# Routing a mixture of experts from the raw residual: where the norm is applied, how the first pair's rows are picked, and where the block arithmetic stands

## The chip, the cores and the metric

One core of one Trainium2 chip runs the whole step in one launch. The time is device microseconds of one execution. TensorE (PE), VectorE (DVE), ScalarE (ACT), GpSimd (POOL) and SyncE (SP) have instruction streams of their own and meet only in semaphores; SP here issues the large loads. TensorE's clock has two levels, 2.4 GHz (the profile's granted clock 1.00) and 1.2 GHz (0.50).

## The reference, cut to what matters

The part that the change touches begins with the merge of the two attention branches and ends with the experts' first blocks:

```python
x = x + jnp.einsum('btd,de->bte', gate_nsa * y_nsa + gate_diff * y_diff, w_out)
h = rmsnorm(x, norm_ffn).reshape(b * t, D_MODEL)          # 320 rows (256 + 64) of 1024
...
logits = (h @ w_router + b_router).astype(jnp.float32)    # 32 experts
top_val, top_idx = lax.top_k(logits, TOP_K)               # 4 per row
gates = jax.nn.softmax(top_val, axis=-1)
...
gu = x_e @ w_gate_up[e] + b_gate_up[e]                    # 1024 -> 2048, f32
act = (up + 1.0) * gate * jax.nn.sigmoid(SWIGLU_ALPHA * gate)
return act @ w_down[e] + b_down[e]                        # 1024 -> 1024, f32
```

All is f32. An expert's weights are 8.39 MB (gate and up) and 4.19 MB (down), 32 experts are 403 MB.

## The kernel before, in words

The kernel is written engine by engine; each engine's order is that of its Python function, and nothing reorders it. The 320 rows stand in three tiles t = 0, 1, 2 of 128, 128 and 64 rows.

**Merge and projection.** `branch_products` gives six (tile, half) pieces v, DVE multiplies and adds each (`m_done`), TensorE transposes it (`tp`, 4 transposes), ACT takes the left half out of PSUM and DVE the right one, into `mT`. Then five output projections `out_proj(v)` of 8 f32 matmuls each (v = 4 holds both halves of the 64-row tile) end in `z_full`.

**Norm and router.** DVE adds each piece to the residual `x5` (`x2_done`), ACT squares and takes the root, DVE writes the normed rows `hn[t]`; TensorE transposes them, the gains `gffn` are multiplied in on the way out of PSUM (`hT6`), and 24 matmuls (`logits`) give the logits.

**Dispatch.** DVE finds the four experts of each row (`max`, `max_index`, the one-hot `oh`, the mask `msk16`). 12 small matmuls with triangles and ones give each row's rank within its expert (`rk`) and the experts' counts (`cc`). From these DVE works out `dest`, the slot of each (row, choice) in blocks of `BS` = 64 rows, with the arithmetic for experts that fill more than one block (`steps_over`, `nb`, `ovb`). A `pick` matrix of a pair of experts, rows by 128 slots, has a 1 where a row goes to a slot: `pick_rows` builds it from `dest` in 12 DVE instructions. `picked(p)` multiplies it with `hn` (pick is the stationary operand, 6 matmuls of 512 columns), ACT copies the result to `hg`, `rows_t` transposes it in 8 pieces, and `rows_out` multiplies by the gains into `hTm`, two halves of 64 slots, one for each expert of the pair.

**Experts.** For each pair of experts: `gate_up(i, u)` (32 matmuls, weights streamed as the moving operand, plus 4 for the biases), DVE and ACT apply the activation, `acts_t` transposes, `down(i, u)` (16 matmuls plus 2), and the results are added back to `x5` through a `spread` matrix. `slot_marks` gives the row numbers and gates of the slots. Both gate-and-up buffers of the pair are one buffer `gu_w` in four chunks of two k-steps: SP may load chunk c of the next expert when the matmuls that read it are done (`e_used`). SP's queue:

```python
sp.wait_ge(z_full, 5)
for h in range(2):
    down_weights(sp, 0, 0, h)
sp.wait_ge(bias_ready, 1)
for h in range(2):
    down_weights(sp, 1, 1, h)
for c in range(4):
    sp.wait_ge(e_used, c + 1)
    gate_up_weights(sp, 1, c)
...
for c in range(4):
    sp.wait_ge(e_used, 5 + c)
    gate_up_weights(sp, 2, c)
```

So expert 0's gate-and-up weights come right behind the branch products, the first four down pieces behind the last projection, expert 1's behind the k-steps of `gate_up(0, 0)`, and expert 2's behind those of `gate_up(0, 1)`; every later load is released in the same way.

## Time and profile before

| | us |
|---|---|
| median of 3 runs | 1601.38 (1599.15 to 1603.20) |
| the profiled execution, its own time | 1600.19 |
| its span in the trace | 1598.5 |
| TensorE matmul busy in it | 1453.9 (91%) |
| DVE, ACT, POOL busy | 483.1, 288.2, 101.9 |
| bytes moved | 507.55 MB, mean 318 GB/s |

The time of the profiled execution is 1.7 us above its span; both belong to the same run. Times in the rows are from the start of the span. An f32 matmul leaves two records in the trace (a transpose or a bf16 matmul leaves one), so counts there are twice those of the code. Busy time says little about limits here: what counts is which stream the last pieces of work wait for.

### The profile page before, as it was taken

The page shows a single profiled execution, that of the slowest core. Times are in us where ns is not written, and L with a number is a line of the kernel's source. Part 1 is how long each engine was busy: PE and PEld are TensorE (multiplying, and loading weights), DVE is VectorE, ACT ScalarE, POOL GpSimd, SP SyncE. Part 2 cuts the span into 40 slices and gives each one's busy share as a digit, 9 for nine tenths or more (in the row PEclk, how much of TensorE's full clock was granted, in tenths as well). Part 3 has the DMA queues.
Part 4 walks back from the last instruction along what each step waited for, and adds up shares of the span by engine and source line. Part 5 has one row for each costly group of instructions (what it writes and reads, how often), then busy time and mean ns, then how long its engine had stood idle before and what let it go on. Part 6 is the DMA issues. An engine that isn't in the chain of part 4 may idle for free.

```text
span 1598.5 us, 21368 instructions
## 1 busy us (share of the span) xinstructions
PE 1453.9 (91%) x7498; PEld 655.7 (41%) x7498; DVE 483.1 (30%) x1097; ACT 288.2 (18%) x613; POOL 101.9 (6%) x217
## 2 busy tenths in 40 slices
PE   5998988988878995899999999999999999999996
PEld 3446554765656443333333333333333333333332
DVE  1113463334343355323132132122222212313214
ACT  2003333333343211010110111110110110010102
POOL 1002002432410000000000000000000000000000
PEclk9997999989989996899999999999999999999998
DMA  7217735665766855589999999999999999999993
GB/s 245 105 53 202 263 93 183 207 204 158 240 179 196 251 220 210 210 361 430 427 428 430 428 427 431 428 427 430 428 427 430 428 427 430 429 427 428 430 426 123
DMA packets 97210, 507.55 MB, mean 318 GB/s; under 512 B 28898, under 2 KB 43714, under 8 KB 72034
## 3 DMA queue, kind: packets, MB, share of 16 engines
q1 hardware_dynamic: 89090, 483.28, 75.7%
q0 software_dynamic: 8064, 23.60, 4.6%
q8 instruction: 25, 0.41, 0.1%
q14 instruction: 31, 0.25, 0.0%
HBM read 500.35 MB, written 10.62 MB: 320 GB/s over the span
## 4 chain that ended last, share of the span: by engine, by line
PE 64%; DMA 18%; DVE 5%; SPq 5%; issue 5%; ACT 2%; DVEq 0%; ACTq 0%
PE PS L1269 20%; DMA arena<-in_w_gate_up 18%; PE PS L1296 9%; PE PS L1243 6%; PE PS L343 5%; PE PS L1870 3%; PE PS L1235 2%; PE PS L1190 2%; PE PS L529 2%; PE PS L1049 2%; SPq L410 2%; PE PS L599 2%; SPq L415 1%; PE PS L352 1%; PE PS L1814 1%
## 5 line engine op out<-in xcount | busy, mean ns | idle before, releaser
L1269 PE MATMUL PS<-arena 128*64 128x512 f32 x2048 | 459.1, 597 | 25.7 <-DMA arena<-in_w_gate_up 23.4
L1269 PEld LDWEIGHTS PS<-arena 128*64 128x64 f32 x2048 | 142.3, 137 | 311.7 <-issue 262.5
L1296 PE MATMUL PS<-arena 128*64 128x512 f32 x1024 | 227.4, 597 | 3.2 <-DVE arena L1689 2.3
L1648 DVE TENSOR_SCALAR arena<-PS 128x512 f32<-128x512 f32 x32 | 22.1, 691 | 501.4 <-PE PS L1278 485.7
L1296 PEld LDWEIGHTS PS<-arena 128*64 128x64 f32 x1024 | 72.4, 138 | 151.3 <-issue 148.6
L529 PE MATMUL PS<-arena 128*128 128x128 f32 (+1 forms) x624 | 98.8, 300 | 37.5 <-ACT arena L762 13.7
L1243 PE MATMUL PS<-arena 128*128 128x512 f32 (+1 forms) x192 | 94.4, 635 | 9.4 <-DVE arena L1596 8.1
L529 PEld LDWEIGHTS PS<-arena 128*128 128x128 f32 (+1 forms) x624 | 72.8, 150 | 61.3 <-ACT arena L762 19.7
L1235 PE MATMUL PS<-arena 128*128 128x512 f32 (+1 forms) x192 | 79.4, 618 | 6.0 <-ACT arena L1438 6.0
L343 PE MATMUL PS<-arena 128*128 128x512 f32 (+1 forms) x192 | 79.6, 576 | 0.6 <-ACT arena L2055 0.6
L1153 POOL COPY arena<-arena 96x64 bf16 (+1 forms) x34 | 7.9, 234 | 1042.0 <-PE PS L1301 954.8
L1618 DVE TENSOR_TENSOR arena<-PS,arena 128x512 f32<-128x512 f32 x34 | 23.3, 687 | 165.1 <-PE PS L1251 160.1
L1423 ACT ACTIVATE arena<-arena 128x512 f32<-128x512 f32 x32 | 20.1, 630 | 273.0 <-DVE arena L1648 273.0
L762 ACT ACTIVATE arena<-PS 128x512 f32<-128x512 f32 (+2 forms) x96 | 51.1, 545 | 77.9 <-PE PS L529 77.5
L1430 ACT ACTIVATE arena<-PS 128x512 f32<-128x512 f32 x32 | 19.1, 597 | 248.0 <-PE PS L1286 248.0
L1437 ACT ACTIVATE arena<-PS 64x512 f32<-64x512 f32 x32 | 18.9, 590 | 230.8 <-PE PS L1301 229.2
L1243 PEld LDWEIGHTS PS<-arena 128*128 128x128 f32 (+1 forms) x192 | 35.4, 197 | 61.2 <-issue 52.9
L1870 PE MATMUL PS<-arena 128*128 128x512 f32 x128 | 59.9, 621 | 0.0
L599 PE MATMUL PS<-arena 128*128 128x252 f32 x256 | 55.1, 376 | 0.0
L343 PEld LDWEIGHTS PS<-arena 128*128 128x128 f32 x192 | 37.2, 195 | 42.4 <-issue 40.1
L2037 ACT ACTIVATE arena<-PS 128x512 f32<-128x512 f32 (+12 forms) x50 | 23.4, 489 | 153.0 <-PE PS L343 54.5
L599 PEld LDWEIGHTS PS<-arena 128*128 128x128 f32 x256 | 48.3, 190 | 5.6
(279 smaller groups left out, 1318.9 us busy)
## 6 DMA issues: line engine op xcount, KB each, us to landing
arena<-in_w_gate_up SPq DMA_DIRECT2D x128, 2048.0 KB, 22.2
arena<-in_w_down SPq DMA_DIRECT2D x64, 2048.0 KB, 21.8
arena<-in_w_in SPq DMA_DIRECT2D x9, 2048.0 KB, 11.7
arena<-in_cache_diff_k SPq DMA_DIRECT2D x64, 256.0 KB, 4.6
arena<-in_cache_diff_v POOLq DMA_DIRECT2D x64, 256.0 KB, 4.3
arena<-in_cache_sel_kv SPq DMA_DIRECT2D x64, 128.0 KB, 2.2
arena<-in_cache_cmp_kv POOLq DMA_DIRECT2D x64, 64.0 KB, 4.2
arena<-in_cache_cmp_kv SPq DMA_DIRECT2D x64, 64.0 KB, 2.8
```

What stands on the lines that cost most here:

```text
L343: last = nc.tensor.matmul(bank(proj_bank(q, 2 * s + t))[:, 0:w], xnT[:, k, 128 * t:128 * t + 128], chunk_at(j)[:, k, 0:w], start=(k == 0), ...
L410: return eng.value_load(ptab[0:1, bass.ds(i * (2 * NPAGE) + (b * NPAGE + pg), 1)], min_val=0, max_val=NPOOL - 1)
L529: last = nc.tensor.transpose(bank(n % 2)[0:c, col:col + r], src, order[0:r, 0:r])
L599: last = nc.tensor.matmul(bank(2)[:, 4 * NCC * c:4 * NCC * (c + 1)], w1[:, c, l, :], cmpT[:, 2 * c:2 * c + 2, :, l % (CS // 2), 2 * l // C ...
L762: copy = lambda d, s: nc.scalar.activation(d, s, ACT.Copy)
L1049: last = nc.tensor.matmul(bank(BRANCH_BANK[v] + half)[p:p + r], src[:, k, 128 * t:128 * t + r], w[:, k, 512 * nh:512 * nh + 512], start=(k ...
L1190: last = nc.tensor.matmul(bank(2 + v)[p:p + r], mT[:, k, 128 * t:128 * t + r], w_out[:, k, 512 * nh:512 * nh + 512], start=(k == 0), stop= ...
L1235: last = nc.tensor.matmul(out, spread[:, 128 * t:128 * t + ROWS[t]], ypair[:, 512 * h:512 * h + 512], start=True, stop=True)
L1243: last = nc.tensor.matmul(bank(h), pick[0:ROWS[t], t], hn[t][0:ROWS[t], 512 * h:512 * h + 512], start=(t == 0), stop=(t == 2))
L1269: last = nc.tensor.matmul(bank(2 + role + 2 * u)[64 * h:64 * h + 64], hTm[:, k, BS * u:BS * u + BS], gu_w[:, k, D * role + 512 * h:D * rol ...
L1296: last = nc.tensor.matmul(bank(6 + u)[64 * h:64 * h + 64], aT[u][:, c % 4, 64 * (c // 4):64 * (c // 4) + 64], down_w[u][c // 4][:, c % 4, ...
L1870: last = nc.tensor.matmul(bank(7), xnT[:, k, 128 * t:128 * t + 128], chunk_at(j)[:, k], start=(k == 0), stop=(k == KD - 1))
```

## The change

Six edits, all between the branch products and the second pair of experts:

1. **Router from raw rows.** TensorE transposes `x5` itself (`x2_t`), not the normed rows. The router weights are multiplied by the gains once (`wr` times `gffn_kp`, a second load of the norm's weights in another layout; `w_router` is loaded in that layout too, rows of 128 bytes in place of 1 KB). The factor 1/rms is applied to the logits in one DVE instruction, `scalar_tensor_tensor`. ACT writes `hn`, off that path.
2. **Order of the tiles.** Merge, transposes and projections are interleaved; the projections run in the order v = 0, 1, 4, 2, 3 (`Z_ORDER`) and the tiles in the order 0, 2, 1 (`T_ORDER`), so that tiles 0 and 2 are transposed, routed and ranked before the last projection ends.
3. **First pair from ranks.** `pick` of the first pair compares each row's rank in experts 0 and 1 with the slot number (`marked_ranks`, `first_rows`); neither `dest` nor the block arithmetic is needed.
4. **Rows stationary.** `first_pick` takes `hn` as the stationary operand and `pick` as the moving one, 8 matmuls of 128 columns for each tile, so the picked rows come out transposed, in banks 4 and 5 that two matmuls with zeros have opened; the ACT copy and the 8 transposes of the first pair are gone.
5. **Block arithmetic later.** `blocks_over`, `dest`, the pair marks and the block lists stand on DVE behind `rows_out` of the first pair; TensorE runs `blocks_over` between k-steps of `gate_up(0, 0)` and `slot_marks` behind `rows_t(1)`, and reads the number of extra pairs behind `down(0, 0)`.
6. **Small ones.** The bias splitting on DVE (`bias16`, `mid16`) is moved into the merge; two dummy activations load ACT's tables early; some buffers have other addresses.

```diff
             load(sp, "late", gffn, io["norm_ffn"].rearrange("a (p k) -> p (a k)", k=KD))
-            load(sp, "late", wr, io["w_router"][0].rearrange("(p k) e -> p k e", k=KD))
+            load(sp, "late", gffn_kp, io["norm_ffn"].rearrange("a (k p) -> p (a k)", p=128), allow_slow_non_contiguous=True)
+            load(sp, "late", wr, io["w_router"][0].rearrange("(k p) e -> p k e", p=128))
...
+            def first_pick(t, ks=range(KD)):
+
+                pe.wait_ge(hn_ready, T_ORDER.index(t) + 1)
+                pe.wait_ge(pick_ready, T_ORDER.index(t) + 1)
+                for k in ks:
+                    last = nc.tensor.matmul(bank(4 + k // 4)[:, 128 * (k % 4):128 * (k % 4) + 128], hn[t][0:ROWS[t], 128 * k:128 * k + 128], pick[0:ROWS[t], t],
+                                            start=False, stop=(t == 1 and k % 4 == 3))
                 return last
...
+            out_proj(2)
+            for half in range(2):
+                x2_t(2, half)
+            for half in range(2):
+                logits(0, half)
+            out_proj(3, range(3))
+            x2_t(1, 0)
+            for half in range(2):
+                logits(2, half)
+            out_proj(3, range(3, 7))
             pe.wait_ge(msk_ready, 1)
...
+            out_proj(3, range(7, KD))
+            logits(1, 0)
+            first_pick(0, range(4))
+            x2_t(1, 1)
+            first_pick(0, range(4, KD))
+            logits(1, 1)
+            first_pick(2)
+            pe.wait_ge(msk_ready, 2)
...
+            first_pick(1).then_inc(x_tp, 1)
...
-            picked(0)
-            rows_t(0)
             pe.wait_ge(bias_ready, 1)
             pe.wait_ge(x_out, 1)
-            gate_up(0, 0)
-            slot_marks()
-            m_out_done(pe, 12)
-            pe.wait_ge(blocks_ready, 1)
-            more = pe.value_load(novi[0:1, 0:1], min_val=0, max_val=NBLK_OVER // 2)
+            gate_up(0, 0, blocks_over, 1)
             pe.wait_ge(x_out, 2)
             picked(1)
             rows_t(1)
+            slot_marks()
             gate_up(0, 1, lambda: acts_t(0, 0))
             down(0, 0)
+            pe.wait_ge(blocks_ready, 1)
+            more = pe.value_load(novi[0:1, 0:1], min_val=0, max_val=NBLK_OVER // 2)
...
+            def marked_ranks(t):
+
+                st.own()
+                op(V.scalar_tensor_tensor, rank1[:, t], bank(3 if t % 2 else 2)[:, NE * t:NE * t + NE], 1.0, msk16[:, NE * t:NE * t + NE], ALU.add, ALU.mult)
+
+            def first_rows(t, p):
+
+                st(V.tensor_tensor(pick[:, t].rearrange("p (e s) -> p e s", e=2), slot1.unsqueeze(1).to_broadcast([128, 2, BS]),
+                                   rank1[:, t, 2 * p:2 * p + 2].unsqueeze(2).to_broadcast([128, 2, BS]), ALU.is_equal), pick_ready if p == 0 or t == 2 else None)
...
+            past(dve, x_tp, 1)
+            for u in range(2):
+                rows_out(st, u, 4)
```

How the instructions stand on TensorE before, from the projections to the block arithmetic's two products (L1190 is a projection, L1171 a transpose, L1201 a logit product, L1223 and L1225 ranks and counts, L1228 and L1229 the two products; the picked rows, six of 512 columns, and their eight transposes follow; the number behind x is how many such instructions follow each other):

```order
L1190 MATMUL PS<-arena 128x512 x32
L1171 MATMUL PS<-arena 128x128 x8
L1190 MATMUL PS<-arena 64x512 x16
L1171 MATMUL PS<-arena 128x128 x8
L1201 MATMUL PS<-arena 128x32 x8
L1171 MATMUL PS<-arena 128x64 x8
L1201 MATMUL PS<-arena 128x32 x8
L1201 MATMUL PS<-arena 64x32 x8
L1223 MATMUL PS<-arena 128x32 x9
L1225 MATMUL PS<-arena 32x1 x3
L1228 MATMUL PS<-arena 128x32
L1229 MATMUL PS<-arena 128x1
```

The same engine after the change, from k-steps 3 to 6 of the last projection to the last ranks; two small count products and the last eight `first_pick` follow (L1198 projection, L1177 transpose, L1213 logits, L1271 the zeros, L1222 ranks, L1237 `first_pick`):

```order
L1198 MATMUL PS<-arena 128x512 x4
L1271 MATMUL PS<-arena 128x512 x2
L1222 MATMUL PS<-arena 128x32 x3
L1198 MATMUL PS<-arena 128x512
L1213 MATMUL PS<-arena 128x32 x4
L1237 MATMUL PS<-arena 128x128 x4
L1177 MATMUL PS<-arena 128x128 x4
L1237 MATMUL PS<-arena 128x128 x4
L1213 MATMUL PS<-arena 128x32 x4
L1237 MATMUL PS<-arena 128x128 x8
L1222 MATMUL PS<-arena 128x32 x3
```

Only a third of the logits and of the picking stands behind the last projection product now, and no product of 512 columns.

DVE behind the rank matmuls before (L1558 takes the ranks out of PSUM; L1522 is the helper `op` of the block arithmetic, L1597 and L1596 are `pick_rows` of the first pair):

```order
L1558 COPY arena<-PS 128x128
L1522 COPY arena<-PS 32x1
L1522 TENSOR_SCALAR arena<-arena 32x1
L1522 SCALAR_TENSOR_TENSOR arena<-arena 32x1 x3
L1569 COPY arena<-arena 32x128
L1522 TENSOR_SCALAR arena<-arena 128x32
L1522 SCALAR_TENSOR_TENSOR arena<-arena 128x32 x3
L1522 TENSOR_SCALAR arena<-arena 128x96
```

And after, behind the last rank matmuls (L1567 is `op` now, L1654 `first_rows`, L1679 the gates' subtraction, L1699 `rows_out`):

```order
L1567 SCALAR_TENSOR_TENSOR arena<-PS,arena 128x32
L1654 TENSOR_TENSOR arena<-arena 128x128
L1679 TENSOR_TENSOR arena<-arena 128x12
L1683 COPY arena<-PS 128x2x32
L1567 COPY arena<-PS 32x1
L1567 TENSOR_SCALAR arena<-arena 32x1
L1567 SCALAR_TENSOR_TENSOR arena<-arena 32x1 x3
L1694 COPY arena<-arena 32x128
L1699 TENSOR_TENSOR arena<-PS,arena 128x8x64 x2
L1654 TENSOR_TENSOR arena<-arena 128x128 x3
```

Two instructions now stand between the last ranks and the last pick matrix, and the arithmetic on `dest` has gone behind the rows of the first pair.

## Rows read from the trace of the kernel before

**Rows 1.** The page: the span, and GB/s in its 40 equal slices.

```profile
span 1598.5 us, 21368 instructions
...
GB/s 245 105 53 202 263 93 183 207 204 158 240 179 196 251 220 210 210 361 430 427 428 430 428 427 431 428 427 430 428 427 430 428 427 430 429 427 428 430 426 123
```

**Rows 2.** Windows: stretch, busy by engine, then granted clock, DMA share, GB/s.

```profile
612.00:624.00 12.00, 10.88 (x61) 10.43 (x60) 3.75 (x17) 3.36 (x9) 0.41 (x2) 0.50 1.00 429
...
628.00:632.00 4.00, 1.01 (x4) 0.93 (x4) 3.46 (x18) 0.00 (x0) 0.00 (x0) 0.50 0.02 8
...
680.00:684.00 4.00, 4.00 (x22) 1.62 (x22) 0.69 (x1) 0.00 (x0) 0.00 (x0) 1.00 0.01 4
...
684.00:688.00 4.00, 4.00 (x21) 1.40 (x18) 0.00 (x0) 0.00 (x0) 0.00 (x0) 1.00 0.75 262
...
1100.00:1500.00 400.00, 383.96 (x1662) 133.35 (x1660) 94.60 (x197) 40.71 (x69) 3.28 (x14) 1.00 1.01 428
```

**Rows 3.** Timeline of SP's queue: start, duration, load.

```profile
606.91 2.04 SPq L1068 DMA_DIRECT2D arena<-in_w_down  x4
...
656.64 0.33 SPq L1065 DMA_DIRECT2D arena<-in_w_gate_up  x1
...
684.28 0.33 SPq L1065 DMA_DIRECT2D arena<-in_w_gate_up  x1
```

**Rows 4.** Timeline of TensorE from the projections to `gate_up(0, 1)`.

```profile
567.75 1.02 PE L1171 MATMUL PS<-arena 128*128 128x128 f32 x8 [3.03 <-DVE arena L1484]
...
599.78 7.09 PE L1190 MATMUL PS<-arena 128*64 128x512 f32 x32
...
617.41 5.47 PE L1201 MATMUL PS<-arena 128*128 128x32 f32 x32
...
626.91 0.76 PE L1223 MATMUL PS<-arena 128*128 128x32 bf16 x9 [4.04 <-DVE arena L1551]
...
638.55 8.55 PE L1243 MATMUL PS<-arena 128*128 128x512 f32 x12 [8.14 <-DVE arena L1596]
...
651.25 15.65 PE L1269 MATMUL PS<-arena 128*64 128x512 f32 x64 [2.32 <-issue]
...
667.27 3.01 PE L1259 MATMUL PS<-arena 128*128 128x52 f32 x24
...
671.54 7.28 PE L1243 MATMUL PS<-arena 128*128 128x512 f32 x12 [1.26 <-issue]
...
679.51 1.15 PE L1251 MATMUL PS<-arena 128*128 128x128 f32 x8 [0.69 <-ACT arena L1413]
...
680.59 7.09 PE L1269 MATMUL PS<-arena 128*64 128x512 f32 x32
```

**Rows 5.** Timeline of TensorE elsewhere: the same kinds of work at full clock.

```profile
207.37 1.16 PE L1902 MATMUL PS<-arena 128*128 128x128 f32 x8 [0.75 <-ACT arena L2037]
...
221.00 3.58 PE L1902 MATMUL PS<-arena 128*128 128x128 f32 x16 [2.60 <-ACT arena L2037]
...
717.82 5.61 PE L1243 MATMUL PS<-arena 128*128 128x512 f32 x12
...
731.95 1.98 PE L1235 MATMUL PS<-arena 128*128 128x512 f32 x4 [0.26 <-ACT arena L1438]
...
788.14 1.98 PE L1235 MATMUL PS<-arena 128*128 128x512 f32 x4 [0.26 <-ACT arena L1438]
```

**Rows 6.** Timeline of DVE: bias split, first of the choice, last of the marks, `rows_out`.

```profile
571.96 3.35 DVE L1491 TENSOR_TENSOR arena<-arena 96x3072 f32<-96x3072 f32 x1
...
623.01 0.23 DVE L1540 TENSOR_TENSOR arena<-PS,arena 128x64 f32<-128x64 f32 x1 [3.16 <-PE PS L1201]
...
642.21 0.64 DVE L1612 TENSOR_SCALAR arena<-arena 128x104 f32<-128x104 f32 x3
...
650.47 1.28 DVE L1618 TENSOR_TENSOR arena<-PS,arena 128x512 f32<-128x512 f32 x2
```

**Rows 7.** The last of three loads of `b_down`, issued at 539.0: time to landing.

```profile
DMA to landing us min/median/max: 13.9/13.9/13.9
```

More of the change, by code:

```diff
@@ new lines, in pe_merge @@
+            out_proj(2)
[5 more added lines that the diff above has]
+            x2_t(1, 0)
+            for half in range(2):
+                logits(2, half)
+            out_proj(3, range(3, 7))
+            pe.wait_ge(msk_ready, 1)
+            for h in range(2):
+                nc.tensor.matmul(bank(4 + h), ones16[0:32], zero16, start=True, stop=False)
+            ranks(0, 0)
@@ new lines, in pe_merge @@
+            ranks(2, 0)
+            ranks(2, 2).then_inc(rk_full, 1)
+            out_proj(3, range(7, KD))
[6 more added lines that the diff above has]
+            pe.wait_ge(msk_ready, 2)
+            for s in T_ORDER:
+                ranks(1, s)
+            for s in T_ORDER:
+                total(s)
+            for s in T_ORDER:
+                last = count(s)
```

348 lines of the change are left out of this document (200 added, 148 removed).

## Prediction

> **What bounds the kernel now.** I read the page first, then the windows from 600 us on, then the timelines of SP, TensorE and DVE over that stretch. The page's GB/s row has two parts: uneven until slice 18, then 426 to 431 in every slice but the last [rows 1]. The window from 1100 to 1500 says why: the DMA share is 1.01 at 428 GB/s while TensorE is busy 383.96 of 400 us [rows 2]. The experts' weights are the bound there. A pair of experts moves 25.17 MB, at 428 GB/s 58.8 us; TensorE needs 56.2 us for a pair, from the combine at 731.95 to the one at 788.14 [rows 5]. TensorE has 2.6 us a pair to spare and follows the loads.
>
> So the end is set by when the stream of weights becomes unbroken, plus the bytes still to come. SP's timeline and the 4 us windows give that moment. The first four down pieces are issued at 606.91 and are in by 628, where the queue falls to 8 GB/s; expert 1's first chunk waits for `gate_up(0, 0)` and is issued at 656.64; from 680 to 684 the engines move 4 GB/s, because expert 2's first chunk waits for the second k-step of `gate_up(0, 1)`, and is issued at 684.28 [rows 2, 3]. From there on nothing breaks. Behind that chunk stand 30 experts' weights, 377.5 MB, which the change leaves alone. What it is worth is therefore how much earlier than 684.28 the second k-step of `gate_up(0, 1)` ends, as long as the loads in front of it are done.
>
> TensorE's timeline from 607 shows what stands before it: logits at 617.41, ranks at 626.91 after 4.04 us of waiting, the first pair's rows at 638.55 after 8.14 us of waiting for DVE's `pick_rows`, the gate products at 651.25, marks at 667.27, `gate_up(0, 1)` at 680.59 [rows 4]. From 612 to 624 the granted clock is 0.50, the 1.2 GHz level, after the wait that followed the last projection [rows 2].
>
> **The change, part by part.** Three stretches, each against the trace.
>
> *A, to the last projection product.* Before, TensorE ran dry at 564.72 (567.75 less the wait of 3.03) with the branch products and three of six transposes done [rows 4]; the projections ended at 606.9. Now it has work throughout. Left at 564.7 are three transposes of four pieces (8 take 1.02 to 1.15, so 0.55 each: 1.7), five projections at 7.05 (7.09 for the one at full clock: 35.2), five transposes of `x5` (2.8), the logits of tiles 0 and 2 (32 records; 24 like them take 3.01 in `slot_marks`, so 0.125 each: 4.0), and the zeros and three ranks (an estimate of 0.8 from nine such in 0.76 at the low clock) [rows 4]. Sum 44.5, end 609.2, 2.3 us later than before. What lies beside it: the bias split on DVE, two instructions of 3.35 and three shorter, now stands between the merges. DVE waits for the bias loads there, and `merge(3)` to `merge(5)` are queued behind. The last landed at 539.0 + 13.9 = 552.9 [rows 7]; the split's first half (1.75 + 3.35 [rows 6]) ends about 558, the last merge about 572, when TensorE wants it. The new `gffn_kp` load and the cut-up `w_router` stand ahead of the bias in the queue. If they cost up to 4 us, TensorE waits 1 to 2 us; below, nothing.
>
> The Trainium skill, "DMA: Bandwidth & Descriptors", Specifications, puts line rate at 512 bytes a piece or more, and both new loads are below it (4 and 128 bytes). That speaks against the layout; the price by this trace stays inside the 4 us above, and no row here shows the page's threshold.
>
> *B, from there to the first gate product.* Before: 606.9 to 651.25, 44.3 us. Now TensorE's list is half the logits of tile 1 (1.0), half of `first_pick(0)` (8 records of 128 columns: 1.16 [rows 5]), a transpose (0.55), the other half (1.16), the logits' other half (1.0), `first_pick(2)` (2.3): 7.2, to 616.4. DVE's choice for tile 1 runs under `first_pick(2)`: for three tiles it took 3.9 (623.01 to the ranks' start at 626.91), for one I take 1.7, as its compare and reduce shrink with the tiles [rows 4, 6]; it may cost the full 3.9, then TensorE waits 1.6 (it ends at 614.1 + 3.9 in place of 616.4). Ranks, totals and counts: 1.0. DVE marks and compares: two instructions near 0.23 and 0.3, with issue 0.6. `first_pick(1)` 2.3. `rows_out` of the first half 0.64, with issue 0.75 [rows 6]. Start at 616.4 + 1.0 + 0.6 + 2.3 + 0.8 = 621.1. B is 11.9 us where it was 44.3. Gone from the path are the block arithmetic and `pick_rows` (627.67 to 638.55, 10.9 us), six products of 512 columns (8.55), a copy and eight transposes (from 647.1, 4.15 with DVE's rows), and most of the logits and transposes (611 to 623).
>
> *C, from the first gate product to the second k-step of `gate_up(0, 1)`.* Before 651.25 to 684.28, 33.0 us. Now 14.1 (twice 7.09) for the gate products, 0.6 for the two products of the block arithmetic, 0.4 biases, 5.6 for `picked(1)` at full clock [rows 5], 0.7 until ACT's copy, 1.15 transposes, 3.0 marks, 3.5 for two k-steps: 29.0. The first gate products took 15.65, 1.55 over twice 7.09, as the clock was partly low [rows 4]; I keep half, 0.8. End of C: 621.1 + 29.8 = 650.9. The register read ahead of `picked(1)`, a wait of 1.26 [rows 4], goes behind `down(0, 0)`, where TensorE is ahead of the loads and it costs nothing.
>
> The arithmetic moved behind `rows_out` is hidden if the marks are ready before `slot_marks`. Before, DVE took from the ranks' end at 627.67 to 642.85 for all of it, `pick_rows` too: 15.2 us [rows 4, 6]. Begun behind the second `rows_out` (621.8) and 1.4 us of `first_rows` and gates, it is ready by 638.4; TensorE comes to `slot_marks` at 621.1 + 22.6 = 643.7. The cover is 5 us at least, and more by the `pick_rows` that are gone; without it each late microsecond would be one on the path.
>
> *The loads.* Four down pieces from 609.2 take 8.39 MB / 428 GB/s = 19.6, to about 629; expert 1's chunks follow without a break, their matmuls being done from 625 on, to about 649. Expert 2's first chunk is issued at 650.9: a gap of 2 us is left of one of 28 and one of 8.
>
> *The sum.* 684.3 - 650.9 = 33.4 us. The profiled execution took 1600.19 (span 1598.5), so 1566.8; the median of the runs shown, 1601.38, is 1.2 above it, so 1568.0.
>
> **The rivals.** *Low clock through B.* The granted clock was 0.50 from 612 to 624 although TensorE was busy 10.88 of 12 us with logits and transposes [rows 2]: such work did not raise it. If it also lets it fall, `first_pick` costs 3.58 for 16 records in place of 2.3 [rows 5]: 2.6 for two of them, 0.5 for the rest, 0.8 more in the first gate products, 1.7 in `picked(1)`. Gain 27.8, time 1573.6. Against it: B begins at full clock and its waits are 0.6 to 0.8 us, where the low stretch before began behind the wait that followed the projections' end at 606.87 [rows 4]. The Trainium skill, "TensorE: Matmul & The Clock Gate", PE-mode transpose, says a transpose doesn't count as busy for the clock; that would favour this rival, and the row from 612 to 624 agrees. Chance 0.2.
>
> *A longer chain.* B is 30 hand-overs. Half a dozen of them 0.5 late, DVE's choice at its upper bound (1.5), the bias late (1.5): 6 us, 1574. Chance 0.12.
>
> *The loads cap it.* If TensorE is quicker than I sum, expert 2 can't be loaded before 649, or 647 if the projections end at 607 as before. Gain at most 37, time 1564.4. That is the near edge of my own case.
>
> *The wait only moves.* If the marks came 15 us later than summed (a DVE wait on `ov_full` or the exponential's table load in the wrong place), `slot_marks` would hold `gate_up(0, 1)`; a late mark of 10 to 15 beyond the cover leaves a gain of 18 to 23, 1578 to 1583. The order speaks against it: `blocks_over` stands at the second k-step, 4 us in. Chance 0.05.
>
> *Slower.* The loop's buffers (`hTm`, `g1` to `av`, `aT`, `ypair`) have other addresses. If that slowed TensorE or the landing weights so that a pair took over 58.8 + 33.4/15 = 61.0 us, the gain would be spent; TensorE's 56.2 would have to grow by 4.8. At 62 us a pair the time is 1568 + 15 × 3.2 = 1616. The loop's instructions are the same, so 0.03. That the order does not free the path at all (1600) gets 0.02.
>
> **The numbers.** My own case, 1564 to 1571, has 0.58. The range 1562 to 1578 reaches from the cap with 2 us of scatter (the runs shown differ by 4) over the cold clock and the longer chain, and leaves out under 0.2. A change under 0.3%, 4.8 us, can't be told from none here. Faster 0.95, same 0.02, slower 0.03.
>
> **What would show it.** Right: the first gate product (L1336) near 621, `gate_up(0, 1)` near 647, the load of expert 2's first chunk near 651 and no window under 400 GB/s behind it; the granted clock 1.00 to about 615; the last projection product near 609; DVE's marks ready before 640. Wrong: a window with 0.50 between 605 and 625 (low clock); TensorE waiting more than 1 us on DVE behind the ranks (long chain); pairs longer than 58.8 us in the loop (slower); a gap in the loads behind 651.

## The result, and the profile after

The changed kernel took 1558.53 us (median of 4 runs, 1556.62 to 1561.83), the kernel before 1600.27 (4 runs, 1596.43 to 1603.20): ratio 0.9743, 95% interval 0.9714 to 0.9772, 41.7 us less. Forecast were 1568.0 us and a range of 1562 to 1578. The sign was right, the time lies 3.5 us below the range. The profiled execution took 1560.01 us, its span 1558.0, 40.5 less than the span of before. Of all executions in this document one stands far off, 5113.32 us of six for the kernel with the load early alone; the time given for it is the median of the other five.

The page after, the span and GB/s in 40 slices (as [rows 1]) and the costliest group, the gate products, with its idle time at the end:

```profile
span 1558.0 us, 21396 instructions
...
GB/s 252 108 54 191 266 98 156 199 238 170 222 160 233 244 281 192 414 429 427 429 429 427 429 429 427 429 429 427 429 429 427 429 429 427 429 429 427 428 429 128
...
L1336 PE MATMUL PS<-arena 128*64 128x512 f32 x2048 | 457.7, 596 | 24.3 <-DMA arena<-in_w_gate_up 23.5
```

Counted from 0, the full rate begins in slice 17, with 414 GB/s already in slice 16; before it began in slice 18, with 361 in slice 17. Of TensorE's 24.3 us of idle time ahead of gate products 23.5 are put down to the weights (23.4 of 25.7 before): they still bound the loop. The windows, with the columns of [rows 2]:

```profile
612.00:616.00 4.00, 3.31 (x16) 3.12 (x15) 1.35 (x7) 1.43 (x2) 0.00 (x0) 0.63 1.02 438
616.00:620.00 4.00, 3.86 (x19) 1.55 (x19) 3.42 (x16) 0.00 (x0) 0.00 (x0) 1.00 0.97 418
...
644.00:648.00 4.00, 4.00 (x22) 1.18 (x18) 0.00 (x0) 0.00 (x0) 0.00 (x0) 1.00 0.82 299
...
1100.00:1500.00 400.00, 384.10 (x1674) 132.99 (x1672) 98.02 (x202) 40.03 (x68) 3.02 (x13) 1.00 1.01 428
```

The two holes in the stream, from 628 and from 680 before, have become one short one: 299 GB/s from 644 to 648. From 1100 to 1500 the rate is the same, 428 GB/s. The granted clock is 0.63 on average from 612 to 616, just ahead of the first gate product, and 1.00 from 616. SP's timeline (as [rows 3]): down pieces, expert 1's first chunk, expert 2's first chunk.

```profile
604.06 1.94 SPq L1073 DMA_DIRECT2D arena<-in_w_down  x4
...
619.82 0.33 SPq L1070 DMA_DIRECT2D arena<-in_w_gate_up  x1
...
644.95 0.33 SPq L1070 DMA_DIRECT2D arena<-in_w_gate_up  x1
```

Expert 2's first chunk is issued at 644.95 in place of 684.28, 39.3 us earlier; the gain of the span is 40.5. TensorE's timeline (as [rows 4]; L1198 projection, L1177 transpose, L1213 logits, L1237 `first_pick`, L1336 gate product, L1326 `slot_marks`):

```profile
561.72 0.66 PE L1177 MATMUL PS<-arena 128*128 128x128 f32 x4
562.21 7.03 PE L1198 MATMUL PS<-arena 128*128 128x512 f32 x16
569.18 0.71 PE L1177 MATMUL PS<-arena 64*128 64x64 f32 x8
569.82 14.15 PE L1198 MATMUL PS<-arena 128*128 128x512 f32 x48
583.90 1.09 PE L1177 MATMUL PS<-arena 128*128 128x128 f32 x8
584.83 7.03 PE L1198 MATMUL PS<-arena 128*128 128x512 f32 x16
591.79 0.71 PE L1177 MATMUL PS<-arena 64*128 64x64 f32 x8
592.43 1.97 PE L1213 MATMUL PS<-arena 128*128 128x32 f32 x16
594.24 2.82 PE L1198 MATMUL PS<-arena 128*128 128x512 f32 x6
596.89 0.60 PE L1177 MATMUL PS<-arena 128*128 128x128 f32 x4
597.42 1.12 PE L1213 MATMUL PS<-arena 128*64 128x32 f32 x16
598.47 3.70 PE L1198 MATMUL PS<-arena 128*128 128x512 f32 x8
...
602.90 1.13 PE L1198 MATMUL PS<-arena 128*128 128x512 f32 x2
603.87 0.97 PE L1213 MATMUL PS<-arena 128*128 128x32 f32 x8
...
611.74 3.57 PE L1237 MATMUL PS<-arena 128*128 128x128 f32 x16 [0.70 <-DVE arena L1654]
616.14 3.65 PE L1336 MATMUL PS<-arena 128*64 128x512 f32 x16 [0.83 <-issue]
...
620.25 10.52 PE L1336 MATMUL PS<-arena 128*64 128x512 f32 x48
...
638.42 2.91 PE L1326 MATMUL PS<-arena 128*128 128x52 f32 x24
641.26 7.09 PE L1336 MATMUL PS<-arena 128*64 128x512 f32 x32
```

The waits of 4.04 and 8.14 us that stood ahead of ranks and picked rows in [rows 4] are gone, and so is a third one of before, ahead of the transposes of the normed rows (TensorE's timeline of before):

```profile
611.08 2.10 PE L1171 MATMUL PS<-arena 128*128 128x128 f32 x8 [4.21 <-ACT arena L1388]
```

Two of 0.70 and 0.83 are left. DVE's marks are ready at 628.7, 9.7 us ahead of `slot_marks` at 638.42, and DVE alone waited for the bias loads (DVE's timeline of after):

```profile
551.21 1.76 DVE L1567 CAST arena<-arena 96x3072 bf16<-96x3072 f32 x1 [2.50 <-DMA arena<-in_b_down]
...
628.11 0.64 DVE L1752 TENSOR_SCALAR arena<-arena 128x104 f32<-128x104 f32 x3
```

### The profile page after: what moved, and what is told of

It reads as the page before. It is cut to its first block, busy times and chain, and to the rows that moved or that the text cites. A ratio compares the mean times of both kernels' runs of the same rounds, so it can differ in the third digit from the quotient of the medians.

```text
span 1558.0 us, 21396 instructions
## 1 busy us (share of the span) xinstructions
PE 1437.8 (92%) x7528; PEld 650.1 (42%) x7528; DVE 475.2 (31%) x1084; ACT 292.1 (19%) x609; POOL 101.8 (7%) x217
## 4 chain that ended last, share of the span: by engine, by line
PE 69%; DMA 19%; DVE 5%; ACT 3%; issue 3%; SPq 1%; ACTq 0%; DVEq 0%
PE PS L1336 21%; DMA arena<-in_w_gate_up 18%; PE PS L1363 9%; PE PS L1310 5%; PE PS L343 5%; PE PS L599 3%; PE PS L529 3%; PE PS L2000 3%; PE PS L1302 3%; PE PS L1198 2%; PE PS L1054 2%; PE PS L352 1%; PE PS L572 1%; PE PS L1944 1%; ACT arena L762 1%
## 5 line engine op out<-in xcount | busy, mean ns | idle before, releaser
L1336 PE MATMUL PS<-arena 128*64 128x512 f32 x2048 | 457.7, 596 | 24.3 <-DMA arena<-in_w_gate_up 23.5
L1336 PEld LDWEIGHTS PS<-arena 128*64 128x64 f32 x2048 | 141.3, 137 | 308.9 <-issue 259.5
L529 PEld LDWEIGHTS PS<-arena 128*128 128x128 f32 (+1 forms) x624 | 73.5, 151 | 61.2 <-ACT arena L762 20.9
L1302 PE MATMUL PS<-arena 128*128 128x512 f32 (+1 forms) x192 | 79.4, 618 | 6.0 <-ACT arena L1506 6.0
L1310 PE MATMUL PS<-arena 128*128 128x512 f32 (+1 forms) x180 | 84.2, 609 | 0.0
L343 PE MATMUL PS<-arena 128*128 128x512 f32 (+1 forms) x192 | 78.6, 571 | 0.6 <-ACT arena L2185 0.6
L1699 DVE TENSOR_TENSOR arena<-PS,arena 128x512 f32<-128x512 f32 x34 | 23.3, 687 | 164.5 <-PE PS L1318 157.0
L2167 ACT ACTIVATE arena<-PS 128x512 f32<-128x512 f32 (+12 forms) x50 | 23.4, 488 | 151.2 <-PE PS L343 53.4
```

The source lines that it names most:

```text
L343: last = nc.tensor.matmul(bank(proj_bank(q, 2 * s + t))[:, 0:w], xnT[:, k, 128 * t:128 * t + 128], chunk_at(j)[:, k, 0:w], start=(k == 0), ...
L529: last = nc.tensor.transpose(bank(n % 2)[0:c, col:col + r], src, order[0:r, 0:r])
L1302: last = nc.tensor.matmul(out, spread[:, 128 * t:128 * t + ROWS[t]], ypair[:, 512 * h:512 * h + 512], start=True, stop=True)
L1310: last = nc.tensor.matmul(bank(h), pick[0:ROWS[t], t], hn[t][0:ROWS[t], 512 * h:512 * h + 512], start=(t == 0), stop=(t == 2))
L1336: last = nc.tensor.matmul(bank(2 + role + 2 * u)[64 * h:64 * h + 64], hTm[:, k, BS * u:BS * u + BS], gu_w[:, k, D * role + 512 * h:D * rol ...
L2167: copy = lambda d, s: nc.scalar.activation(d, s, ACT.Copy)
```

## How the span divides

Four points cut every trace into stretches that can be compared: the last DVE addition ahead of the merge (L942), the issue of the down pieces (the last projection product's end), the first gate product, the end of the span. The first of them, DVE's timeline, of before and then of the first, second and third run of the changed kernel:

```profile
532.05 0.43 DVE L942 TENSOR_TENSOR arena<-arena 128x256 f32<-128x256 f32 x1
```

```profile
529.82 0.43 DVE L942 TENSOR_TENSOR arena<-arena 128x256 f32<-128x256 f32 x1
```

```profile
534.64 0.43 DVE L942 TENSOR_TENSOR arena<-arena 128x256 f32<-128x256 f32 x1
```

```profile
531.88 0.43 DVE L942 TENSOR_TENSOR arena<-arena 128x256 f32<-128x256 f32 x1
```

The six edits of the change stand behind that point, and the changed kernel alone shows 4.8 us of scatter there. All kernels, in us. Time and ratio are from the timed runs, each ratio against the kernel before as it was timed beside it (1600.27 with the first run, 1598.96, 1599.70 and 1599.84 with the later ones); the stretches are from the one profiled run of each. A starts at the merge here.

| kernel | time | ratio, 95% | merge to down issue (A) | to first gate product (B) | from it to the end |
|---|---|---|---|---|---|
| before | 1600.27 | | 74.9 | 44.3 | 947.3 |
| changed | 1558.53 | 0.9743 [0.9714, 0.9772] | 74.2 | 12.1 | 941.9 |
| changed, second | 1562.82 | 0.9765 [0.9745, 0.9785] | 74.2 | 10.5 | 941.8 |
| changed, third | 1561.85 | 0.9763 [0.9749, 0.9776] | 74.2 | 10.5 | 942.2 |
| delay ahead of the gate product | 1569.01 | 0.9808 [0.979, 0.9826] | 74.2 | 17.6 | 941.9 |
| delay behind `down(0, 0)` | 1566.93 | 0.9801 [0.978, 0.9822] | 74.3 | 12.1 | 945.3 |
| arithmetic first | 1572.01 | 0.9825 [0.9806, 0.9845] | 74.2 | 20.9 | 943.1 |
| router from normed rows | 1566.78 | 0.9799 [0.9781, 0.9816] | 73.8 | 15.7 | 941.8 |
| projections first | 1570.30 | 0.9815 [0.9798, 0.9831] | 68.1 | 26.1 | 942.0 |
| rows moving | 1568.65 | 0.9807 [0.9791, 0.9824] | 73.6 | 18.1 | 941.8 |
| second half moved up, load early | 1560.98 | 0.9761 [0.9745, 0.9777] | 74.2 | 10.5 | 941.1 |
| three parts undone | 1583.01 | 0.9905 [0.9885, 0.9926] | 73.2 | 32.9 | 942.5 |
| `down(0, 0)` moved up, load early | 1560.62 | 0.9759 [0.9745, 0.9774] | 74.3 | 11.9 | 938.7 |
| load early alone | 1562.58 | 0.9766 [0.9751, 0.978] | 74.3 | 12.1 | 941.9 |

The 40.5 us of the two spans are 2.2 ahead of the merge (scatter), 0.6 in A, 32.3 in B, 5.4 behind.

## The experiments

### A delay on either side of the first gate-up product

Eight f32 products of 512 columns into an idle bank, about 7.1 us of TensorE (7.11 in the trace). They compute nothing that is used.

```diff
             pe.wait_ge(x_out, 1)
+            for _ in range(8):
+                nc.tensor.matmul(bank(1), ident, hn[0][:, 0:512], start=True, stop=True)
             gate_up(0, 0, blocks_over, 1)
```

> The changed kernel with eight f32 matmuls of 512 columns (7.0 us of TensorE in the changed kernel's trace) ahead of the first gate product; their result isn't used. The theory of the stream says that the end follows the issue of expert 2's first gate-and-up chunk (644.8 us in the changed kernel) by 913 us: the issue comes at 651.8 and the time is 1558.5 + 7.0 = 1565.5. The rival, that the gain came from TensorE's total work and clock and the order in front hardly counts, says that a delay is made up in the loop, where TensorE has 2.6 us a pair to spare: 1558.5, at most 1560.

In the second kernel the eight products stand behind `down(0, 0)`, ahead of the wait for `blocks_ready`, into bank 7.

> The same eight matmuls, 7.0 us, behind the first down product instead of ahead of the first gate product. The theory of the stream: expert 2's chunk is issued at 644.8 as before, the weights in the queue keep it busy to about 674, and the next release (667.0 in the changed kernel) may come 7 us late: the time is 1558.5 to 1559.5. A theory by which any delay of TensorE in this stretch counts: 1565.5.

Ahead of the gate product the delay shows in full. TensorE's timeline of that kernel (L1422 is the delay; its down pieces are issued at 608.08):

```profile
618.66 7.11 PE L1422 MATMUL PS<-arena 128*128 128x512 f32 x16 [0.87 <-DVE arena L1701]
625.69 3.65 PE L1336 MATMUL PS<-arena 128*64 128x512 f32 x16
```

B grows from 10.5 to 17.6, 7.1 us against the traces at full clock, as this one was (5.5 against the first trace), and the rest stays at 941.9. Behind `down(0, 0)` it should have vanished in TensorE's lead over the loads; it cost 3.4 us, so neither the expectation nor its rival was right. SP's timeline of the second kernel:

```profile
661.35 3.76 SPq L1073 DMA_DIRECT2D arena<-in_w_down  x2
675.65 11.46 SPq L1070 DMA_DIRECT2D arena<-in_w_gate_up  x4
```

Expert 3's first chunk is issued at 675.65, 14.30 behind the down pieces; in the changed kernel that is 667.03 - 659.95 = 7.08, so it is 7.2 late, of which half is made up. In the first pairs TensorE has no lead yet that would swallow 7 us. The mechanism holds, but that work behind `down(0, 0)` costs nothing, as the prediction says of the register read, holds only up to some 3.7 us (an estimate: 7.1 less 3.4).

### One part undone at a time

**The block arithmetic first**: DVE does `dest`, the marks and the block lists' start ahead of `rows_out`, TensorE `blocks_over` ahead of the gate product.

```diff
+            blocks_over()
             pe.wait_ge(bias_ready, 1)
             pe.wait_ge(x_out, 1)
-            gate_up(0, 0, blocks_over, 1)
+            gate_up(0, 0)
```

> One edit undone: DVE does the block arithmetic up to the marks before the first pair's rows come out of PSUM, and TensorE runs the two products of the block arithmetic right behind the last pick. In the changed kernel that arithmetic takes 617.2 to 628.7, less a wait of 0.7, so 10.8 us; begun at 612.8 it ends at 624, the rows are out at 625 and the gate products start near 625.3 in place of 616.1. Without the two products inside, the second k-step of the second gate product is 8.5 us later, up to 10.5 if the wait lowers the clock: 1567 to 1569. If the arithmetic's place doesn't matter, 1558.5.

> The changed kernel once more, unaltered, on the chip of the three others: 1558.5, the first merge within 3 us of 536, and the issue of expert 2's first chunk 913 us ahead of the end. If the part ahead of the merge had become faster by the change, the first merge would be near 536 in every kernel with the change and near 538 in the kernel before; if it only scatters, it differs by 2 us among these four.

The changed kernel took 1562.82 here, and its merge came 4.8 us later than in the first trace, not within 3; among the four kernels of this round it lies 3.4 us apart. So the part ahead scatters, and it was not the change that had made it faster. The times expected for this round stood on 1558.5 and came out too low; against 1562.82 the delay in front cost 6.2 us (7.0 expected), the one behind 4.1 (0 to 1, or 7), arithmetic first 9.2 (8.5 to 10.5).

Arithmetic first costs 8.8 us in B against the first trace of the changed kernel, 10.4 against the second, and 1.3 behind, as the clock is still low when the gate products begin. `first_pick(1)` met the low clock there (3.60 us), as in the first trace, so 8.8 is the like-for-like figure. TensorE's timeline shows the wait that the change had taken away:

```profile
618.50 0.36 PE L1296 MATMUL PS<-arena 32*128 32x1 f32 x2
627.97 4.62 PE L1336 MATMUL PS<-arena 128*64 128x512 f32 x12 [9.11 <-issue]
```

9.11 us without work stand between the block arithmetic's second product and the first gate product; DVE is busy with `dest` and the marks until 627.2 and takes the first rows out only then.

**The router from normed rows**: transposes and logits take `hn` again, so the 64-row tile's stand behind its norm and behind the last projection.

```diff
-                pe.wait_ge(x2_done, 2 * j + (half + 1 if t == 1 else 2))
-                tp(6 + 2 * j + half, [(x5[0:r, t, 128 * k:128 * k + 128], r * (k % 4)) for k in range(4 * half, 4 * half + 4)])
+                pe.wait_ge(hn_ready, j + 1)
+                tp(6 + 2 * j + half, [(hn[t][0:r, 128 * k:128 * k + 128], r * (k % 4)) for k in range(4 * half, 4 * half + 4)])
```

> The first part of the change undone alone: transposes and logits take the normed rows again, the logits are added to the bias without the norm, w_router is read in its old layout; ranks, picked rows, products with stationary rows and the place of the block arithmetic stay as changed. The 64-row tile then stands behind its own norm and its scaled copy, so its transposes and logits move behind the last projection product. Theory (the experts' weights are read without a gap from a moment that the first pair's start sets; every microsecond of start is one of time): the first gate product starts 3 to 5 us later counted from the last projection product, expert 2's first chunk is issued 3 to 5 us later, the time is 3 to 5 us above that of the changed kernel, the span minus that issue stays at 913. Rival (the gain came from the block arithmetic and the picked rows alone, the norm's place is hidden): within 1 us of the changed kernel. Rival (the early part counts more, the router of the other two tiles also waits): more than 7 us above.

**The projections first**: the routing of the two full tiles goes behind the last projection product.

```diff
+            out_proj(2)
+            out_proj(3)
             arrived(pe, "late")
             for half in range(2):
                 x2_t(0, half)
-            out_proj(2)
...
```

> The changed kernel with the transposes, logits and ranks of the two full tiles put behind the last projection product, where they stood between projections. Nothing is removed. The last projection product ends about 6 us earlier (the work taken out from between), and the down weights of the first expert are issued as much earlier; the first gate product comes 3 to 5 us later than in the changed kernel, as the choice for two tiles (some 7 us on VectorE with ranks between) is no longer covered by projections. Theory (the start of the first gate product decides, with the loads' stream behind it): issue of expert 2's first chunk 3 to 5 us later, time 3 to 5 us above the changed kernel, 5 to 7 if TensorE's granted clock falls in the longer wait. Rival (the loads decide, since the down weights start earlier): time 0 to 3 us below the changed kernel.

**The rows moving**: the marks stationary, six products of 512 columns, the copy on ACT, eight transposes.

```diff
-            first_pick(1).then_inc(x_tp, 1)
+            for t in range(3):
+                for h in range(2):
+                    last = nc.tensor.matmul(bank(h), pick[0:ROWS[t], t], hn[t][0:ROWS[t], 512 * h:512 * h + 512], start=(t == 0), stop=(t == 2))
...
```

> The changed kernel with the first pair's rows picked the old way: the marks are stationary and the normed rows move (6 products of 512 columns), ScalarE copies the picked rows to SBUF, TensorE turns them in 8 transposes; the zero products that open the two banks are left out. Router, ranks and the place of the block arithmetic stay as changed. Most of the products with stationary rows lie in the changed kernel before the last marks, where TensorE waits anyway; moved behind them they cost 6 x 0.22 to 0.43 us of products, a copy of 1 to 2 us a half with the way to ScalarE and back, and 8 transposes of 0.07 to 0.15 us, against 1 to 2 us of products for the 64-row tile: 3 to 7 us. Theory: expert 2's first chunk is issued 3 to 7 us later and the time is 3 to 7 us above the changed kernel, span minus issue 913. Rival (the picking's form is hidden by the arithmetic on VectorE that runs beside it): within 1 us.

The router costs 3.6 us in B against the first trace, 5.2 against those at full clock, the moving rows 6.0 and 7.6. In the router's kernel `first_pick(1)` took 3.65, the low price, so 3.6 is the like-for-like figure. The projections first shorten A by 6.1 and lengthen B by 14.0, 7.9 more than they save; expected were 3 to 5, or up to 7. In time the three lie 4.0, 5.8 and 7.5 us above the changed kernel's second run (router, moving rows, projections first), which was not timed beside them. A window of the last one shows a part of why it is above:

```profile
608.00:620.00 12.00, 8.64 (x45) 7.27 (x46) 5.02 (x19) 4.01 (x6) 0.00 (x0) 0.50 1.00 429
```

With no projections between them to cover the hand-overs, TensorE waits for DVE (1.53 and 2.84 us are the longest of these waits), and transposes, logits, ranks and first picks run at the low level for 12 us, as transposes and logits did from 612 to 624 before [rows 2]. In all three the rest of the span stays at 941.8 to 942.0: what A and B gain or lose is all there is.

### Three parts undone together

Normed router, moving rows and arithmetic first in one kernel; early routing of the two full tiles and the choice of the first pair from ranks stay.

```diff
-                pe.wait_ge(x2_done, 2 * j + (half + 1 if t == 1 else 2))
+                pe.wait_ge(hn_ready, j + 1)
...
-            first_pick(1).then_inc(x_tp, 1)
+            last.then_inc(pick0, 1)
...
-            gate_up(0, 0, blocks_over, 1)
+            gate_up(0, 0)
```

> Three parts undone together: router from normed rows, the first pair's rows picked with the normed rows moving, and the block arithmetic ahead of the first gate product. What stays of the change: the router of the two full tiles between projections, and the first pair picked from ranks. Measured one at a time, the stretch from the last projection product to the first gate product was 12.1 us in the changed kernel (10.5 with TensorE's clock at 1.00 throughout), 15.7 with the normed router, 18.1 with the rows moving, 20.9 with the arithmetic first. Theory (each lengthens one serial chain, and from the first gate product on 942 to 943 us follow in all of them): the parts add, the stretch is 30.5 to 34 us, the time 18 to 24 us above that of the changed kernel. Rival (each of the three pays for the same low-clock stretch, which comes once): 25 to 29 us, 13 to 17 above. Rival (the arithmetic hides the other two, or they it): under 24 us.

B is 32.9. Added one by one to the first trace the three give 12.1 + 3.6 + 6.0 + 8.8 = 30.5, to the second 10.5 + 5.2 + 7.6 + 10.4 = 33.7: they add to within some 2 us, as links of one chain do. Of the 2.4 us above the first sum 2.0 are a low clock under the late transposes and logits, which took 1.09 and 1.97 us in the router's kernel. TensorE's timeline here:

```profile
609.48 1.48 PE L1178 MATMUL PS<-arena 128*128 128x128 f32 x8 [4.48 <-ACT arena L1482]
610.82 3.62 PE L1214 MATMUL PS<-arena 128*128 128x32 f32 x16
```

The time is 21.2 us above the third run of the changed kernel, of the 38.0 that the change gains there. The other 11.4 us of B up to 44.3 are left to early routing and the choice from ranks together; no run separates the two, and they are a difference of two kernels with other lists in A, so they can't be set against the 14.0 of the projections first.

### Who sets the issue of expert 2's first chunk

Two kernels try to get under the loads. In the first the second half of `gate_up` stands right behind the first, picked rows, transposes and marks behind it, and one down load of expert 1 is issued before the wait for `z_full`.

```diff
             pe.wait_ge(x_out, 2)
+            gate_up(0, 1, lambda: acts_t(0, 0))
             picked(1)
             rows_t(1)
             slot_marks()
-            gate_up(0, 1, lambda: acts_t(0, 0))
...
+            sp.wait_ge(bias_ready, 1)
+            down_weights(sp, 1, 1, 1)
             sp.wait_ge(z_full, 5)
```

> The changed kernel with two moves. (1) The second half of the first pair's gate-up product stands right behind the first half; the picking of the second pair's rows, its transposes and the slot marks come behind it, on all three engines. (2) One of the four down-weight loads (expert 1's second half, 1 MB) is issued before the wait for the last projection product instead of behind it, in the stretch of some 19 us in which the queue has nothing to do. Theory (the end is set by the loads' stream from expert 2's first chunk on; that issue waits for the later of TensorE's second k-step and of the loads in front of it): TensorE's step comes about 7 us earlier and no longer decides, the loads in front end about 34.3 us behind the last projection product instead of 39.2, so the issue comes 5 to 6 us earlier and the time is 4.5 to 6 us below the changed kernel. Rival (a later place in the first pairs binds again, since the second pair's rows come late by what the first pair's came early): 0 to 2 us below. Rival (the early load displaces reads that the projections wait for): not faster.

In this kernel the activations overwrite a table before `slot_marks` has read it, so the experts' outputs go to wrong rows; the amount of work is the same. Expert 2's first chunk is issued at 634.91, 29.1 us behind the down pieces in place of 40.9. The end gains 0.6 to 2.3 us only. A window and SP's timeline show the next gate:

```profile
660.00:664.00 4.00, 4.00 (x22) 1.36 (x20) 2.66 (x10) 0.00 (x0) 0.00 (x0) 1.00 0.68 229
```

```profile
661.85 3.76 SPq L1073 DMA_DIRECT2D arena<-in_w_down  x2
```

Expert 2's down pieces need the buffer that `down(0, 0)` frees, which still stands behind all of the work that was only reordered: 661.85 is 56.0 us behind the down issue, in the changed kernel's three traces it was 55.9, 54.3 and 54.3. The expectation's first rival, that a later place binds again, had it right. The second kernel therefore puts the marks ahead of the second half, and `down(0, 0)` ahead of the second pair's rows:

```diff
+            slot_marks()
             pe.wait_ge(x_out, 2)
-            picked(1)
-            rows_t(1)
-            slot_marks()
             gate_up(0, 1, lambda: acts_t(0, 0))
             down(0, 0)
+            picked(1)
+            rows_t(1)
```

> The changed kernel with the slot marks right behind the first half of the first gate-up product, then its second half and the down product of the first expert, and only then the second pair's rows and their transposes; and with one of the four down-weight loads (1 or 2 MB of expert 1) issued before the wait for the last projection product. The run before it with the second half moved up won 0 to 2 us because the down weights of expert 2 then waited for the down product of expert 0, behind the picked rows; here that product stands 7 us earlier. Theory (the loads' stream is unbroken from the last projection product to the end and alone sets the end, so what is loaded before it is won): no window under 400 GB/s behind 612, and the span minus the last projection product's end 2 to 5 us under the 952.3 of the changed kernel's second run, time 2 to 5 us below it. Rival (TensorE's own work up to the loop, not the loads, sets the end): within 1 us of it.

> The changed kernel with the early down-weight load alone, TensorE's order as changed. Theory (TensorE's second k-step of the first pair's second half decides when expert 2's first chunk is issued, 39.3 to 40.9 us behind the last projection product, and the loads in front, now done by 34 to 37, do not): the gap in front of that chunk is wider, the time within 1 us of the changed kernel. Rival (the loads decide there already): 2 to 4 us below.

> The changed kernel once more, beside the three others. Its two runs so far gave 1558.5 and 1562.8 us against 1600.3 and 1599.0 of the kernel before. In their traces the part ahead of the merge ended up to 5 us apart, and behind the first gate product both took 941.8 us. Theory (that part scatters, whatever the kernel): 1558 to 1563 us, ratio 0.973 to 0.978; from the first gate product to the end of the span 941.5 to 942.2 us; the stretch in front of it 10.5 or 12.1 us, as TensorE's clock stays at 1.00 or falls there.

Now the down pieces of expert 2 are issued at 653.93, 48.6 behind the first ones:

```profile
605.38 1.29 SPq L1073 DMA_DIRECT2D arena<-in_w_down  x3
...
653.93 3.76 SPq L1073 DMA_DIRECT2D arena<-in_w_down  x2
```

```profile
620.00:632.00 12.00, 12.00 (x62) 4.18 (x58) 10.54 (x31) 0.00 (x0) 0.00 (x0) 1.00 0.96 358
632.00:656.00 24.00, 24.00 (x128) 10.17 (x126) 6.19 (x13) 2.07 (x4) 0.00 (x0) 1.00 1.01 430
```

From 632 on nothing breaks; from 620 to 632 the queue waits for `gate_up(0, 0)` and loses 2 us at 358 GB/s, of the 4.9 that the early piece had won (it is half of 4.19 MB, so 2.1 MB, not the 1 MB of the expectation). From the down issue to the end it takes 950.6 us, where the changed kernel's runs took 953.9, 952.3 and 952.7: 1.7 to 3.3 less. That nothing breaks from 612 on was wrong, and against the 952.3 that the expectation names the 1.7 us fall short of the 2 to 5 expected. On the clock of a whole run it is 1560.62 against 1561.85 of the changed kernel beside it, ratios 0.9759 and 0.9763 with intervals that overlap: no difference that can be told, and this kernel does not show that the loads alone set the end. The early load alone changes nothing (941.9, ratio 0.9766); its gap in the stream is wider, as expected:

```profile
640.00:648.00 8.00, 8.00 (x44) 3.67 (x45) 0.00 (x0) 0.21 (x1) 0.00 (x0) 1.00 0.55 203
```

In the second run of the changed kernel, where the clock stayed up, the same place has no gap (expert 2's first chunk is issued at 648.23, 39.3 us behind the down pieces), so that TensorE's step and the loads in front came due together there:

```profile
644.00:648.00 4.00, 4.00 (x22) 1.67 (x23) 0.00 (x0) 0.21 (x1) 0.00 (x0) 1.00 1.01 426
```

## Why the prediction was right, and where it was not

**The mechanism was right.** The end follows from when the weights' stream becomes unbroken, as long as no later release is late. Eight profiles whose B runs from 10.5 to 26.1 us (the changed kernel's three, the delay in front, normed router, projections first, rows moving, load early alone) all end 941.8 to 942.2 us behind the first gate product, and the change gained in span what it gained up to expert 2's first chunk, to 1.2 us.

**Stretch B came out right by luck**: 11.9 forecast, 12.1 in the profile, with a first gate product at 616.1 in place of 621.1 only because it starts earlier. My 11.9 was a sum for full clock, where the same list takes 10.5; the low clock, which I had put into a rival, added 1.6. Most of the excess is in the part up to the last ranks, 7.2 forecast and 6.0 measured (604.06 to the last product of `first_pick(2)`, at 610.0).

**The cover of the arithmetic was right**: at least 5 us forecast, 9.7 measured, with no wait at `slot_marks`. The bias loads delayed DVE by 2.5 us and TensorE not at all. The new layouts of `gffn_kp` and `w_router` cost SP time, but not the end: the issues of `w_router` and of the load behind it took 2.21 and 4.85 us in place of 0.43 each (in the kernel with the normed router, which reads `w_router` in the old layout, the second of them took 0.47 again). So the last bias load was issued 13.6 us behind the merge in place of 6.9, yet DVE was released by it 21.4 us behind the merge, where it had landed at 20.8 before.

**Stretch A failed as a sum.** The time fell below the range, and "Sum 44.5, end 609.2, 2.3 us later than before" is the step that failed. Measured from the merge, A is 0.6 shorter than before, 2.9 less than I summed. The projections were right: 7.05 forecast, two in 14.15 measured. By the starts of the rows above, the logits of tiles 0 and 2 took 1.81 + 1.05 in place of 4.0: with 64 columns stationary a record has half the price, and I had priced all 32 by the 128-row `slot_marks`. The half price was to be read in [rows 4] and [rows 5], where 32 such records of 512 columns take 7.09 and 12 with 128 columns stationary 5.61. The five transposes of `x5` took 0.93 + 0.64 + 0.53 in place of 2.8, the three of the merge 0.49 + 0.64 in place of 1.7. These make 2.4; the list also starts 0.8 us earlier behind the merge (at 561.72) than the 564.72 that I took, and 0.2 go the other way, from the last product to SP's issue.

**Stretch C was 1.0 long**: 29.8 forecast, 28.8 measured (644.95 - 616.14). The 0.8 for a cold start of the gate products was not due (3.65 + 10.52 for the two groups, where twice 7.09 was the price at full clock): the clock was back at 1.00 in the window from 616.

**The part behind the chunk** was taken over from before as 914.2; it is 912.9 to 913.3 in ten of the thirteen profiles of kernels with the change. The others are the one delayed behind `down(0, 0)` and the two in which the second half of `gate_up` was moved up, where a later release decides. The 1.2 lie at the very end. TensorE's timeline of before shows the last down product (8.49 us), of after the same one (7.09):

```profile
1573.46 8.49 PE L1296 MATMUL PS<-arena 128*64 128x512 f32 x32 [2.29 <-DVE arena L1689]
```

```profile
1534.27 7.09 PE L1363 MATMUL PS<-arena 128*64 128x512 f32 x32 [2.29 <-DVE arena L1819]
```

```profile
1570.00:1580.00 10.00, 7.71 (x32) 2.69 (x30) 7.29 (x20) 1.78 (x3) 0.00 (x0) 0.83 0.00 0
```

The window is of before: the granted clock was 0.83 there. In the changed kernel's three profiles that product takes 7.09. That the change has to do with it is not shown.

**The scatter was too small in my range.** The part ahead of the merge ended 2.2 us earlier in the profiled run than before; over three runs of the same kernel it lies 4.8 apart. Together: the span that I summed, 621.1 + 29.8 + 914.2 = 1565.1, less the measured 1558.0 is 7.1, which is 2.2 (scatter) + 2.9 (A) + 1.0 (C) + 1.2 (tail) - 0.2 (B). The 1.2 that I had added for the median of the runs shown did not recur either, and the changed kernel's profiled run was 1.5 slower than its median, less 0.3 by which its time stands further above its span: that makes the 9.5 between 1568.0 and 1558.53. Where the changed kernel was timed again, at 1562.82 and 1561.85, the near edge of 1562 was met once and missed by 0.15 once; the forecast of 1568 was too slow in all three.

**The rivals.** *Low clock through B* was half right: the clock fell in the profile of the changed kernel, and cost 1.6 us, not 5.6, since only `first_pick(1)` met it (3.57 against 2.02 below). The 3.58 in [rows 5] by which it was priced stands at the low level too, 0.57 from 221 to 225, and not at full clock as the heading there says. The Trainium skill, "TensorE: Matmul & The Clock Gate", PE-mode transpose, says that a transpose does not count as busy for the clock in the way that other work does. No run here shows it: the window with the projections first, at 0.50 with TensorE busy 8.64 of 12 us, does not speak against it, but logits, ranks and picks stand in it too, and one list with one group of four transposes ran at both levels. *Loads cap it* was nearer than my own case in its time, and wrong as a cap: its 37 us of gain took 607 for the projections' end, and the down pieces were issued at 604.06, 0.6 of it by A and 2.2 by scatter. It has to be read as a distance: the loads in front, 16.78 MB at 428 GB/s, end 39.2 us behind the down issue, and expert 2's chunk was issued 39.3 behind in both traces at full clock, 40.9 in the first.

## What to carry to other kernels

Where a queue of large loads is the bound and small work precedes it, find the instruction that releases the first load of the unbroken stretch, and sum only the chain to it; whatever is not on that chain (DVE's arithmetic here) is worth moving behind it. Take prices per shape from rows with the same number of stationary columns, and give the range at least the scatter that parts ahead of the change show. A buffer released earlier pays only up to the next one in the queue: moving one release by 12 us gained 0.6 to 2.3, and moving the next one too brought the gain to 1.7 to 3.3, less than runs of one kernel differ by.

## What the runs showed of the hardware that was not expected

The same list of instructions met the low clock in some executions and not in others. `first_pick(1)` and its surroundings, TensorE's timeline, of the changed kernel's second run:

```profile
616.56 2.02 PE L1237 MATMUL PS<-arena 128*128 128x128 f32 x16 [0.70 <-DVE arena L1654]
```

In the first run it took 3.57, after the same wait of 0.70. Of seven profiles with this list unchanged four show B at 11.9 to 12.1 and three at 10.5; the list of instructions ahead was the same in all, and stretch A 74.2 to 74.3 us. Why the clock fell in some of them stays open.

ScalarE's copy that reorders a row while it scales it (`hn`, 1024 f32 elements of each row) takes 2.17 us, where a pass over 512 elements in order takes 0.63, so 1.7 times as long for each element; no run separates the reordering from the scaling. Here it is hidden. ScalarE's timeline of the changed kernel:

```profile
604.87 0.63 ACT L1460 ACTIVATE arena<-arena 128x512 f32<-128x512 f32 x1 [6.74 <-DVE arena L1606]
...
607.70 2.17 ACT L1478 ACTIVATE arena<-arena 128x1024 f32<-128x1024 f32 x1 [0.23 <-DVE arena L1620]
```
